# Latent attention: the values of all heads computed by rows of tokens in four weight units behind the compressed query

## The reference

```python
kv = (c_kv @ w_ukv).reshape(bsz, s_len, B_HEADS, QK_NOPE_DIM + V_HEAD_DIM)
return kv[..., :QK_NOPE_DIM], k_rope, kv[..., QK_NOPE_DIM:]
...
cq = rms_norm(h @ w_dq, q_norm)
q = (cq @ w_uq).reshape(bsz, s_len, B_HEADS, QK_NOPE_DIM + QK_ROPE_DIM)
...
logits = (qn . k_nope + q_rope . k_rope) * scale, causal
p = softmax(logits);  o_h = p @ v_h;  mix = concat(o_h) @ w_o
```

## Time and profile before

| | |
|---|---|
| median of three runs | 1863.21 us (1863.05 to 1863.34) |
| profiled execution | 1861.66 us, its span 1859.7 us |
| PE busy | 1842.6 us (99%) |
| PE weight loads busy | 1693.9 us (91%) |
| DVE busy | 1318.0 us (71%) |
| ACT busy | 914.3 us (49%) |
| GpSimd busy | 53.6 us (3%) |
| latent attention | about 1319 to 1480 us of the span |
| its loop over heads | about 1350 to 1445 us |

### The profile page before, as it was taken

How to read it: one execution, slowest core, us unless ns; L and a number is a source line. 1 busy time by engine, 2 the same in 40 slices (tenths; PEclk the granted TensorE clock), 3 DMA queues, 4 the chain that set the end, 5 groups by cost and what they waited for, 6 DMA issues and landing times.

```text
span 1859.7 us, 31170 instructions
## 1 busy us (share of the span) xinstructions
PE 1842.6 (99%) x12175; PEld 1693.9 (91%) x12175; DVE 1318.0 (71%) x1742; ACT 914.3 (49%) x1386; POOL 53.6 (3%) x51
## 2 busy tenths in 40 slices
PE   8999999999999999999999999999999999999999
PEld 7899988988889899998898999989988898999888
DVE  6888862487656888882288888822888488888623
ACT  6455552355545545562255555622666464455522
POOL 0000000011100000000000000000000000000000
PEclk9999999999999999999999999999999999999999
DMA  6244343232223333333323343333221232343331
GB/s 183 80 113 113 91 115 102 79 90 72 77 57 102 91 91 106 97 104 106 108 57 108 91 113 104 102 98 104 63 63 57 69 91 84 99 112 105 109 102 47
DMA packets 339464, 174.64 MB, mean 94 GB/s; under 512 B 11070, under 2 KB 337836, under 8 KB 339372
## 3 DMA queue, kind: packets, MB, share of 16 engines
q1 hardware_dynamic: 338656, 172.25, 33.0%
q10 hardware_dynamic: 716, 1.11, 0.2%
HBM read 171.24 MB, written 2.10 MB: 93 GB/s over the span
## 4 chain that ended last, share of the span: by engine, by line
PE 85%; DVE 9%; ACT 3%; issue 2%; DMA 0%; POOL 0%; DVEq 0%; SPq 0%; ACTq 0%
PE acc L1881 19%; PE acc L1882 19%; PE acc L1883 19%; PE duo L1881 9%; PE duo L1883 9%; PE duo L1882 9%; DVE wl L1175 2%; DVE xg L1220 1%; DVE mx L1534 1%; PE acc L2147 1%; DVE probT L1555 1%; ACT prob L889 1%; DVE y L1240 1%; ACT wh L641 0%; DVE xT L1247 0%
## 5 line engine op out<-in xcount | busy, mean ns | idle before, releaser
L1881 PE MATMUL acc<-xg,wh 128*128 128x256 f32 (+1 forms) x1040 | 340.4, 327 | 2.4 <-DVE xg L1220 1.0
L1883 PE MATMUL acc<-xg,wl 128*128 128x256 f32 (+1 forms) x1040 | 336.9, 324 | 0.0
L1882 PE MATMUL acc<-xg,wh 128*128 128x256 f32 (+1 forms) x1040 | 336.8, 324 | 0.0
L1175 DVE TENSOR_TENSOR wl<-raw,wh 128x1024 fp32r<-128x1024 f32 (+2 forms) x198 | 228.9, 1168 | 126.5 <-ACT wh L641 126.2
L1882 PE MATMUL acc<-hT,wh 128*128 128x512 f32 (+1 forms) x704 | 255.2, 363 | 0.0
L1881 PE MATMUL acc<-hT,wh 128*128 128x512 f32 (+1 forms) x704 | 255.2, 363 | 0.0
L1883 PE MATMUL acc<-hT,wl 128*128 128x512 f32 (+1 forms) x704 | 255.2, 362 | 0.0
L641 ACT ACTIVATE wh<-raw 128x1024 fp32r<-128x1024 f32 (+2 forms) x198 | 194.4, 1011 | 116.4 <-PE acc L1883 71.8
L1881 PEld LDWEIGHTS acc<-xg,wh 128*128 128x128 f32 x1040 | 197.7, 190 | 20.5 <-issue 3.1
L1883 PEld LDWEIGHTS acc<-xg,wl 128*128 128x128 f32 x1040 | 197.7, 190 | 15.8
L1882 PEld LDWEIGHTS acc<-xg,wh 128*128 128x128 f32 x1040 | 197.9, 190 | 14.9
(11 more groups left out here) (283 smaller groups left out, 4175.6 us busy)
## 6 DMA issues: line engine op xcount, KB each, us to landing
raw<-in_ffn_w_dram SPq DMA_DIRECT2D x238, 512.0 KB, 4.2
raw<-in_ffn_w_dram SPq DMA_DIRECT2D x32, 384.0 KB, 3.4
raw<-in_moba_w_qkv_dram SPq DMA_DIRECT2D x24, 512.0 KB, 3.8
raw<-in_moba_w_o_dram SPq DMA_DIRECT2D x8, 512.0 KB, 3.8
raw<-in_mla_w_o_dram SPq DMA_DIRECT2D x8, 512.0 KB, 3.7
xin<-in_x_dram SPq DMA_DIRECT2D x4, 512.0 KB, 5.4
raw<-in_mla_w_dq_dram SPq DMA_DIRECT2D x4, 512.0 KB, 3.9
raw<-in_mla_w_uq_dram SPq DMA_DIRECT2D x8, 256.0 KB, 2.9
```

The source lines that it names most:

```text
L1175: v.tensor_tensor(wl[:, slot, 0:tiles], raw[:, slot, 0:tiles], f32(wh[:, slot, 0:tiles]), ALU.subtract).then_inc(w_lo, 1)
L1881: t.matmul(dst, w_h, m_h, start=start, stop=False, skip_group_check=onto)
L1882: t.matmul(dst, w_h, m_l, start=False, stop=False, skip_group_check=onto)
L1883: return t.matmul(dst, w_l, m_h, start=False, stop=stop, skip_group_check=onto)
```

## The change

The values of all heads are computed at once, ahead of the heads, with tokens on partitions. Now the latent is the stationary operand (a block of 128 tokens) and the weights are the moving one (512 columns, the value columns of four heads). Four new weight units of 4 tiles each hold them: unit i has the rows 128 (i mod 2) of `w_ukv` and the values of heads 0 to 3 (i below 2) or 4 to 7. For each unit TensorE makes 4 token blocks x 3 products of 512 columns, into eight banks in turn; the results of four heads for a block come out of two units. ScalarE and VectorE split these eight results (`latent_hi`, `latent_lo`) right into the buffers `oM`, in which the output of each head later takes the place of its values.

Gone are, for each head, the value's 2 tiles in the head's unit (which has now 6 tiles and two DMAs), 6 matmuls, the copy on VectorE, the 4 transposes and the split behind them. The splits of the new units stand between those of the compressed query on ScalarE and VectorE; the load of ScalarE's table moves behind them. In the loop the order of odd heads changes: query of head h + 2 ahead of the weighted sum; in even heads the weighted sum stands between rotary unit and query.

```diff
-    MLA_U = [(UT, 1)] * KQ + [(KQ, 2), (UT, 3), (UT, 3)] * (HEADS // 2) + [(UT, 1)] * KD
+    MLA_U = [(UT, 1)] * KQ + [(KH, 1)] * 4 + [(KQ, 2), (KQ + KK, 2), (KQ + KK, 2)] * (HEADS // 2) + [(UT, 1)] * KD
...
-        for st, special in ((1, {4: sco[2], 5: acc[0], 6: aux}), (5, {KQ: sco[1], KQ + 1: sco[2]})):
+        for st, special in ((1, {4: sco[2], 5: acc[0], 6: aux}), (5, {**dict(enumerate((*acc, *sco, aux, *acc))), VM: sco[1], VM + 1: sco[2]})):
...
+            per_head = w_ukv.rearrange("(k p) (h a d) -> p k h a d", p=P, h=HEADS, a=2)
+            for i in range(4):
+                u = U0[5] + KQ + i
+                slot_free(u)
+                sp.dma_start(raw[:, u % SLOTS, 0:KH], per_head[:, i % KK, KH * (i // KK):KH * (i // KK + 1), 1]
+                             ).then_inc(raw_full[u % SLOTS], 16)
...
-                    load(u % SLOTS, KQ + KK, ukv[:, :, 2 * P * h + P:2 * P * (h + 1)])
...
ScalarE
+            def latent_hi(i):
+                g, c = divmod(i, TS)
+                act.wait_ge(*((latent_psum, (TS - 1) * g + c + 1) if c < TS - 1 else (unit_done, u + KQ + KK * (g + 1))))
+                s.activation(latent_part(i, 0), att_banks[5][KQ + i][:].rearrange("p (h d) -> p h d", d=P), COPY
+                             ).then_inc(v_hi, 1)
...
             split(u + 5)
             cq_hi_of(1)
+            split(u + 6)
+            cq_hi_of(2)
+            split(u + 7)
+            cq_hi_of(3)
             load_table(EXP)
-            cq_hi_of(2)
-            cq_hi_of(3)
-            split(u + 6)
+            for i in range(TS):
+                latent_hi(i)
+            split(u + 8)
+            split(u + 9)
+            for i in range(TS, 2 * TS):
+                latent_hi(i)
+            split(u + 10)
...
VectorE
+            def latent_lo(i):
+                dve.wait_ge(v_hi, HEADS + i + 1)
+                v.tensor_tensor(latent_part(i, 1), att_banks[5][KQ + i][:].rearrange("p (h d) -> p h d", d=P),
+                                f32(latent_part(i, 0)), ALU.subtract).then_inc(evacuated, 1)
...
             split(u + 4)
-            cq_lo_of(0)
             dve.wait_ge(var_psum, EV0[N_PRE4] + 1)
             row_sums(xvar[:], 0).then_inc(r_ready, 1)
+            cq_lo_of(0)
             split(u + 5)
-            for m in range(1, KQ):
-                cq_lo_of(m)
+            cq_lo_of(1)
             split(u + 6)
+            cq_lo_of(2)
+            split(u + 7)
+            cq_lo_of(3)
+            for i in range(TS):
+                latent_lo(i)
+            split(u + 8)
+            split(u + 9)
+            for i in range(TS, 2 * TS):
+                latent_lo(i)
+            split(u + 10)
...
-            copy_v(0)
...
-                if nxt:
-                    copy_v(h + 1)
...
-                    v_split(n + 1)
...
TensorE
+            for i in range(4):
+                g, k = divmod(i, KK)
+                w = u + KQ + i
+                pe.wait_ge(w_lo, w + 1)
+                for c in range(TS):
+                    if (i, c) == (0, TS - 1):
+                        pe.wait_ge(r_ready, EV0[N_PRE4] + 1)
+                    dst = att_banks[5][KQ + TS * g + c] if k else att_dst(5, KQ + TS * g + c)
+                    dst, cols = dst[:].rearrange("p (h d) -> p h d", d=P), slice(c * P, (c + 1) * P)
+                    w_h, w_l = wh[:, w % SLOTS, 0:KH], wl[:, w % SLOTS, 0:KH]
+                    t.matmul(dst, ckT[:, 0, k, cols], w_h, start=k == 0, stop=False)
+                    t.matmul(dst, ckT[:, 0, k, cols], w_l, start=False, stop=False)
+                    ins = t.matmul(dst, ckT[:, 1, k, cols], w_h, start=False, stop=k == KK - 1)
...
-            head_part("v", 0).then_inc(head_psum, 1)
             head_part("q", 0).then_inc(unit_done, 1)
-            value_transposes(HEADS, r + mla_rr["v", 0] + 1)
             head_part("q", 1).then_inc(head_psum, 1)
...
-                head_part("k", h + 1).then_inc(head_psum, 1)
-                head_part("v", h + 1).then_inc(unit_done, 1)
-                if h:
+                head_part("k", h + 1).then_inc(unit_done, 1)
+                if h + 2 < HEADS and h % 2 == 0:
+                    gg = (h + 2) // 2
+                    unit(mla_unit(gg), att_dst(5, mla_rr["r", gg]), q_of(gg), KQ)
+                    if h:
+                        values(n - 1)
+                    head_part("q", h + 2).then_inc(head_psum, 1)
+                else:
+                    if h + 2 < HEADS:
+                        head_part("q", h + 2).then_inc(head_psum, 1)
                     values(n - 1)
```

More of the change, by code:

```diff
@@ L361, in yoco_kernel @@
         vT_psum = sem("vT_psum")
+        latent_psum = sem("latent_psum")
         v_hi = sem("v_hi")
@@ L415, in values_of, with latent_part @@
         def values_of(n):
+            if n >= HEADS:
+                return tuple(oM[a][:, n - HEADS].rearrange("p (t d) -> p t d", d=P) for a in range(2))
             return vh[:, n % 2, 0], vh[:, n % 2, 1]
+        def latent_part(i, a):
+            g, c = divmod(i, TS)
+            return oM[a][:, KH * g:KH * (g + 1), c * P:(c + 1) * P]
         def o_of(n, a):
@@ L446, in head_result @@
             if h == 0:
[L447 to L449 removed]
+                return {"k": (head_psum, 1), "q": (unit_done, mla_unit(0, 0) + 1)}[a]
+            return {"q": (head_psum, h + 1), "k": (unit_done, mla_unit(h // 2, h) + 1)}[a]
         @block.sync
@@ L1106, in _ @@
             direct("q", 0, qh[:, 0])
-            v_split(HEADS)
             rotated(0, 0)
             rotated(0, 1)
-            split(u + 7)
-            split(u + 8)
+            split(u + 11)
+            split(u + 12)
             for h in range(HEADS):
@@ L1142, in _ @@
                     o_split(n - 1)
-                if nxt and not turn:
-                    v_split(n + 1)
             probT_split(2 * HEADS - 1, (0, 1, 2))
             o_split(2 * HEADS - 1)
-            out_proj(u + KQ + 12, N_MLA, gain(1, 3, 0))
+            out_proj(u + KQ + 16, N_MLA, gain(1, 3, 0))
             x_update(X_MLA, N_MLA, gain(1, 3, 0), U0[6], gain(1, 4, 0), N_PRE5)
@@ L1847, in _ @@
                     products((h + 2) // 2)
-                if nxt and not turn:
-                    v_split(n + 1)
             probT_split(2 * HEADS - 1, (0, 1, 2))
             o_split(2 * HEADS - 1)
-            out_proj(u + KQ + 12, N_MLA)
+            out_proj(u + KQ + 16, N_MLA)
             x_update(X_MLA, N_MLA, gain(1, 4, 0), U0[6], R0[6])
@@ L2139, in prob_transposes @@
                 for b in pieces:
-                    if b == 1 and (n + 1) % HEADS:
+                    if b == 1 and n + 1 < HEADS:
                         pe.wait_ge(v_lo, n + 2)
@@ L2192, in out_proj @@
                 heads_done(0, 0, HEADS - 3)
-                value_transposes(last, att)
+                if st == 1:
+                    value_transposes(last, att)
                 prob_transposes(last - 1, (0,))
@@ L2295, in head_part @@
             def head_part(a, h, before=None):
-                first, n = {"q": (0, KQ), "k": (KQ, KK), "v": (KQ + KK, KK)}[a]
+                first, n = {"q": (0, KQ), "k": (KQ, KK)}[a]
                 w = mla_unit(h // 2, h)
@@ L2301, in head_part @@
                              before=before)
+            pe.wait_ge(cq_lo, KK)
+            for i in range(4):
[11 more added lines that the diff above has]
+                    ins = t.matmul(dst, ckT[:, 1, k, cols], w_h, start=False, stop=k == KK - 1)
+                    if k == KK - 1 and c < TS - 1:
+                        ins.then_inc(latent_psum, 1)
+                ins.then_inc(unit_done, 1)
             pe.wait_ge(cq_lo, KK + 3)
             head_part("k", 0).then_inc(head_psum, 1)
-            unit(mla_unit(0), att_dst(5, mla_rr["r", 0]), q_of(0), KQ,
-                 before=lambda k: pe.wait_ge(evacuated, r + k + 1))
-            head_part("v", 0).then_inc(head_psum, 1)
+            unit(mla_unit(0), att_dst(5, mla_rr["r", 0]), q_of(0), KQ)
             head_part("q", 0).then_inc(unit_done, 1)
-            value_transposes(HEADS, r + mla_rr["v", 0] + 1)
             head_part("q", 1).then_inc(head_psum, 1)
```

35 lines of the change are left out of this document (15 added, 20 removed).

## The result

The changed kernel takes 1871.8 us in the median of five runs (1870.15 to 1873.43); the kernel before 1863.21. The ratio is 1.0047, with a 95% interval of 1.0033 to 1.0062: slower by 8.6 us. Forecast were 1871.6 us.

The account below looks back on a forecast made before the run. The softmax round of VectorE and ScalarE was taken to bound the loop, not TensorE. +9.6 at the front - 0.44 - 2 x 0.37 = +8.4 us; with 1.55 from profile to median, 1871.6 us, range 1868.5 to 1874.0.

Parts of the forecast that it names:

- What bounds: Loop over heads: the softmax round of VectorE and ScalarE sets the pace, 27.67 us a pair, not TensorE.
- 48 matmuls at the front: Between compressed query and first key: value products take 10.88 us, first key 9.96 us later.
- the old wait of 0.76: Ahead of the first key product, a 0.76 us wait for its weights, forecast to go.
- First rotary chain: Ahead of the first scores: chain of 7.21 us, scores at 1359.25, 9.6 us later, 1.6 of it new wait.
- What the loop gives back: Steady pairs, heads 2-3 and 4-5: 0.37 us each, 0.27 from the weight split and 0.10 from the copy.
- First pair: Heads 0 and 1: gives back 0.44 us, from 0.07, 0.27 and 0.10.
- New waits: Odd heads: query's bank takes 1 us of 3 slack, covered; head 6 waits 2.5 us for normalization.
- The sum: Whole kernel: +9.6 - 0.44 - 2 x 0.37 = +8.4 us; profiled execution 1870.1, median 1871.6.
- Rival 1: In the loop TensorE is the bound: 4.0 us less in all, 1859.2 us; chance 0.05.
- Rival 2: In the loop copy and value split were both on the round: 7.2 us back, +2.4, 1865.6; chance 0.05.
- Rival 4: Value unit waits for split or bank, or rotary chain queues on VectorE: 2 to 4 us more; chance 0.09.
- Rival 3: Clock falls in the new waits: an odd head takes 7.5 us more, in three heads, 1894; chance 0.03.

Follow-up runs that it names:

- e1: The kernel before, with 4 of 6 value matmuls left out for each head: 1862.69 us median.
- e2: The changed kernel, with the next head's key computed twice in odd heads 1, 3 and 5: 1873.42 us median.
- e3: The changed kernel, with one more 0.6 us VectorE product in heads 0, 2 and 4, ahead of the rotary products: 1874.2 us median.
- e4: The changed kernel, with one more 0.6 us VectorE product in heads 0, 2 and 4, behind the rotary products: 1871.58 us median.
- e6: The changed kernel, VectorE making rotary products right behind normalization in even heads, and row maxima ahead of probabilities' and key's low parts: 1865.38 us median.
- e7: The kernel before, VectorE making rotary products right behind normalization in even heads, and row maxima ahead of probabilities' and key's low parts: 1862.48 us median.
- e9: The changed kernel, with the next head's key computed three times in heads 1, 3 and 5 and twice in head 6: 1875.03 us median.
- e10: The changed kernel, with the rotary unit ahead of head 0's key on all three engines: 1869.01 us median.
- e12: The changed kernel itself run again, unchanged: 1870.16, 1870.19, 1871.70, 1873.04 and 1873.63 us.

## Why the prediction was right, point by point

- **What bounds.** Right. The step that mattered was to take the chain of waits over the busy share. e1, e2, e3, e4, e6 and e7 show it from both sides; e9 shows the limit, a wait can be filled only as long as what the round needs stays on time.
- **48 matmuls at the front.** 10.88 us forecast, 10.91 measured (1337.20 to 1348.11), no gap; the old wait of 0.76 went. Splits, banks and DMAs were ready.
- **First rotary chain.** First scores forecast at 1359.25, measured 1359.16; from the rotary unit's last matmul (1351.96) to these scores it took 7.20 us against 7.27. The new wait was forecast as 1.6 from start to start; by that measure it is 1.5 (the last query product starts at 1357.40, so the next would at 1357.63), and 1.37 from modelled end to start. e10 shows that it was the rotary chain.
- **What the loop gives back.** 0.37 for a pair forecast, 0.35 measured (27.67 to 27.32). The split of 768 columns takes 0.95, the middle of its two rows. The reciprocal of odd heads now idles 0.53 us for the exponentials where the copy stood: of the copy's 0.60 only about 0.1 was on the round.

```profile
1412.07 0.18 DVE L1570 RECIPROCAL rsums<-psums 128x4 f32<-128x4 f32 x1 [0.53 <-ACT prob_odd L903]
...
1427.22 0.95 DVE L1199 TENSOR_TENSOR wl<-raw,wh 128x768 fp32r<-128x768 f32 x1
```

- **First pair.** 25.97 from first scores to the second pair before, 25.53 forecast, 25.60 measured.
- **New waits.** The query's bank costs 0.91 of slack in heads 3 and 5 (1 forecast; 0.30 in head 1) and nothing in time; head 6 waits 2.0 us (2.5 forecast).
- **The sum.** +8.4 forecast, +8.5 lowest to lowest. Against its own profiled execution the sum said 1870.1 and the trace shows 1871.72; 1.54 of the 1.6 between is the half-clock piece. That the median was met to 0.2 us is in part luck: I added 1.55 as the distance between profile and median without knowing what it was. It is the price of one half-clock piece. By the mean clocks the median of before has it at the start of the kernel and its profile not at all, and the changed kernel's median has one in the loop: two different events of the same price, not one that was carried over.
- **Rivals 1, 2 and 4** did not come about: the loop did not follow TensorE (e1, e2), the value split's place was free (e4) and the copy's nearly so (0.53 of its 0.60 is idle now), and no value unit waited.
- **Rival 3** was right in kind and wrong in size. The clock did fall behind a new wait, but for 3 us and 1.5 us of time, not for a whole odd head and 7.5. By the mean clocks seven of ten executions of the changed kernel have such a piece in the loop, where none of 54 of before has; so the chance of 0.03 was too low, and the price should have been taken as one short piece for each event. It did not throw the median off only because that of before has a piece of its own, at the start. The Trainium skill, "TensorE: Matmul & The Clock Gate", section "Why this matters for your kernels", warns that idle gaps bring back the half clock. The trace agrees in kind, 0.50 from 1386 to 1389, though the wait just ahead of it is only 1.85 us.

## What to carry to other kernels

An engine that is busy 99% of a stage can still have a shorter round of other engines beside it: follow the chain of waits through one period and compare its length with each engine's own work in that period. Work moved out of such a loop is paid in full where it lands and gives next to nothing back (0.35 us a pair here) until the round is shortened too; put the two edits together (e6: 6.6 us; the reordering alone, e7: nothing). Work put into the wait of such a loop is free only while the round's own pieces stay on time (e2, e9). And in a round the order of instructions on one engine decides: 0.6 us of VectorE work cost 0.6 on one side of the rotary products and 0 on the other.

## What the runs showed of the hardware

- TensorE's clock fell to 0.50 for some 3 us inside a stage whose longest wait is 2.0 us, at different places in different executions: at 1386 in the changed kernel, behind a wait of 1.85 us; at 1455 in e2, behind one of 2.04; from 1358 to 1361 in e1, behind three of 0.43 to 0.80 within 8 us. Each was worth 1.5 to 1.8 us, and they set the levels of the times. What decides in which execution it happens is open.
- At the start of a kernel the granted clock's record can read 1.00 while matmuls run at half rate: in e12 those of 256 columns start 0.21 us apart until 15.1 us, in the kernel before 0.12 apart. The distance between starts is the safer reading there.
